# Expert stage of a routed mixture: the down product of a block placed behind the next block's up product

## What is computed there

```python
def expert_block(args):
    tok, e = args
    xb = xt[tok]
    g = xb @ w_gate[e] + b_gate[e]
    u = xb @ w_up[e] + b_up[e]
    g = jnp.minimum(g, SWIGLU_LIMIT)
    u = jnp.clip(u, -SWIGLU_LIMIT, SWIGLU_LIMIT)
    act = (u + 1) * (g * jax.nn.sigmoid(SWIGLU_ALPHA * g))
    return act @ w_down[e] + b_down[e]
```

## Time and profile before

| | us |
|---|---|
| median of 3 runs (lowest 4122.18, highest 4126.77) | 4125.26 |
| the profiled execution, device time | 4122.54 |
| its span in the trace | 4120.8 |
| TensorE busy over the span (83%) | 3426.4 |
| VectorE busy over the span (48%) | 1973.6 |
| expert stage, from the first gate product to the last down product | 838 to 2091 |

### The profile page before, as it was taken

The page is one execution under the profiler, slowest core; times in us unless marked ns, Lnnn a source line. Parts: engine busy times, 40 slices in busy tenths (PEclk is TensorE's granted clock), DMA queues, the critical chain, the costliest instruction groups (busy, mean ns, idle before and its releaser), DMA issues. The chain is left out here.

```text
span 4120.8 us, 37527 instructions
## 1 busy us (share of the span) xinstructions
PE 3426.4 (83%) x11876; PEld 1539.3 (37%) x11877; DVE 1973.6 (48%) x4086; ACT 659.6 (16%) x1532; POOL 932.9 (23%) x811
## 2 busy tenths in 40 slices
PE   7988998587899979999869845778788788888876
PEld 3345443332233323333335434544333233333332
DVE  5834223422333232232244055656666767667676
ACT  1011121000000000000022111412222222222212
POOL 2000000102222221021220040003444444444443
PEclk9999999699999989999989966899999999999998
DMA  9825333469999995597972000038999999999997
GB/s 333 284 87 200 137 115 114 188 229 408 376 364 366 364 412 233 215 363 283 385 262 98 27 0 0 1 150 345 421 415 412 421 408 408 422 403 422 417 421 327
DMA packets 194149, 1157.36 MB, mean 281 GB/s; under 512 B 25659, under 2 KB 27995, under 8 KB 74356
## 3 DMA queue, kind: packets, MB, share of 16 engines
q1 hardware_dynamic: 97140, 565.17, 35.3%
q0 software_dynamic: 80576, 564.05, 33.5%
q10 hardware_dynamic: 16320, 26.75, 2.1%
HBM read 1128.96 MB, written 48.68 MB: 286 GB/s over the span
## 5 line engine op out<-in xcount | busy, mean ns | idle before, releaser
L2462 DVE SCALAR_TENSOR_TENSOR mod<-q_uv,mix 128x1024 f32<-128x1024 f32 x512 | 627.1, 1225 | 391.5 <-DMA q_uv<-in_peer_uv,q_picks 387.0
L1149 PE MATMUL ps<-wt,e_xT 128*64 128x512 f32 x3200 | 729.4, 609 | 97.7 <-DMA wt<-in_w_exp 96.9
L2167 POOL DMA_INDIRECT q_uv<-in_peer_uv,q_picks x512 | 569.5, 1112 | 1053.9 <-PE ps L2259 720.8
L2259 PE MATMUL ps<-q_uv,q_dg 128*128 128x512 f32 x1024 | 518.7, 663 | 144.5 <-ACT q_dg L2336 144.5
L2259 PE MATMUL ps<-q_uv,tri 128*128 128x512 f32 x1024 | 465.4, 608 | 81.3 <-ACT tri L2336 81.3
L1129 POOL COPY wt<-e_land 128x2048 f32<-128x2048 f32 x124 | 237.7, 1917 | 1019.4 <-DMA e_land<-in_w_exp 1019.4
L1149 PEld LDWEIGHTS ps<-wt,e_xT 128*64 128x64 f32 x3200 | 236.9, 140 | 580.5 <-issue 430.0
L2259 PEld LDWEIGHTS ps<-q_uv,q_dg 128*128 128x128 f32 x1024 | 213.1, 213 | 441.1 <-issue 441.1
L1149 PE MATMUL ps<-wt,e_aT 128*64 128x512 f32 x1600 | 356.0, 597 | 21.5 <-ACT e_aT L1202 21.5
L2259 PEld LDWEIGHTS ps<-q_uv,tri 128*128 128x128 f32 x1024 | 194.9, 194 | 348.0 <-issue 347.9
L454 PE MATMUL ps<-hT,wt 128*128 128x512 f32 x640 | 285.1, 602 | 1.5 <-DVE wt L781 1.5
(11 more groups left out here) (439 smaller groups left out, 3402.7 us busy)
## 6 DMA issues: line engine op xcount, KB each, us to landing
wt<-in_w_exp SPq DMA_DIRECT2D x260, 1024.0 KB, 17.5
e_land<-in_w_exp SPq DMA_DIRECT2D x124, 1024.0 KB, 24.4
wt<-in_w_in_units SPq DMA_DIRECT2D x15, 2048.0 KB, 11.1
mod<-in_w_mod_units SPq DMA_DIRECT2D x48, 512.0 KB, 5.8
scratch_xs<-const_zeros SPq DMA_DIRECT2D x8, 2080.0 KB, 9.4
mod<-in_w_ada_units SPq DMA_DIRECT2D x32, 512.0 KB, 7.5
p_ring<-in_w_in SPq DMA_DIRECT2D x7, 2048.0 KB, 10.6
e_xg<-scratch_xs ACTq DMA_DIRECT2D x104, 128.0 KB, 7.3
```

The source lines that it names most:

```text
L1149: ins = nc.tensor.matmul(ps[64 * h:64 * h + 64, at, :], lhs[:, k % 4, 64 * (k // 4):64 * (k // 4) + 64], wt[:, u, a, h * W:(h + 1) * W], s ...
L2167: pool.indirect_dma_start(out=uv[:, n % NR, :, :].rearrange("p a d -> p (a d)"), out_offset=None, in_=A["peer_uv"], in_offset=bass.Indirec ...
L2259: last = nc.tensor.matmul(acc(t)[:, c, :], dg(n), uv[:, n % NR, 1, c * W:(c + 1) * W], start=fresh, stop=closing)
L2462: dve.scalar_tensor_tensor(junk[:, n % 2, :], uv[:, n % NR, 0, :], 1.0, mix[:, tile_of(k), :], ALU.mult, ALU.mult, accum_out=ap[:, k % 2, ...
```

## The change

Two orders are rewritten and nothing else. TensorE's loop body does the up product of block i before the down product of block i-1:

```diff
                             turn(AT, ut, s_at)
                             pe.wait_ge(s_xg, i * 32 + 64)
                             turn(XT, xg, s_xt)
+                            up(e, b)
                             down(i - 1, before)
-                            up(e, b)
```

```diff
                     dve.tensor_scalar(gt[:, :], gt[:, :], LIMIT, None, ALU.min).then_inc(s_g, 1)
+                    dve.wait_ge(s_mm[7], i * 2 + 4)
+                    dve.wait_ge(s_g, i + 2)
+                    dve.sem_inc(s_go, 1)
+                    link(dve.tensor_tensor(ut[:, :], ps[:, U, :], bias[:, 1, :], ALU.add))
+                    link(dve.tensor_scalar(ut[:, :], ut[:, :], LIMIT, -LIMIT, ALU.min, ALU.max))
+                    link(dve.scalar_tensor_tensor(ut[:, :], ut[:, :], 1.0, gt[:, :], ALU.add, ALU.mult))
+                    dve.wait_ge(s_sig, i + 1)
+                    dve.tensor_tensor(ut[:, :], ut[:, :], sg[:, :], ALU.mult).then_inc(s_act, 1)
                     if not first:
                         scaled(i - 1)
                         dve.wait_ge(s_y, i + 1)
                     dve.sem_inc(s_dve, 1)
                     count[0] += 1
-                    dve.wait_ge(s_g, i + 2)
-                    dve.sem_inc(s_go, 1)
                     dve.stream_shuffle(bias[:, 2, :], raw[:, 2, :], [0] * 32).then_inc(s_shuf, 1)
-                    dve.wait_ge(s_mm[7], i * 2 + 4)
-                    link(dve.tensor_tensor(ut[:, :], ps[:, U, :], bias[:, 1, :], ALU.add))
-                    link(dve.tensor_scalar(ut[:, :], ut[:, :], LIMIT, -LIMIT, ALU.min, ALU.max))
-                    link(dve.scalar_tensor_tensor(ut[:, :], ut[:, :], 1.0, gt[:, :], ALU.add, ALU.mult))
-                    dve.wait_ge(s_sig, i + 1)
-                    dve.tensor_tensor(ut[:, :], ut[:, :], sg[:, :], ALU.mult).then_inc(s_act, 1)
```

## The result

The changed kernel takes 4239.41 us (median of 4 runs, 4238.54 to 4241.59), the kernel before 4126.02. The ratio is 1.0277, with a 95% interval from 1.0259 to 1.0295: 113.4 us slower, where 100.9 was forecast.

A forecast was written before the change was run, and what follows sets the result against it. By turns DMA pace (one-block experts) or TensorE (many-block experts) bounds the kernel. 92.3 + 4.6 + 4.0 - 2.1 + 2.1 = +100.9 us on 4125.3 gives 4226.2; range 4185 to 4262.

The forecast's parts named there:

- The restart: DMA engines, where a several-block expert gives way to the next: up units issued 6.44 us later, behind the s_shuf wait.
- the place of the up product: TensorE, second expert after a several-block one: up product, now next to its weights, waits for them; 3.8 us per change.
- The nine changes: From a several-block expert over one or more one-block experts to the next several-block one: 9 x 10.26 = 92.3 us slower.
- M straight to M: Two places where one several-block expert directly follows another: 2 x 2.3 = 4.6 us slower.
- the start: First blocks of the expert stage: spreading of the down bias stands behind the whole up chain; 4.0 us slower.
- The end: Last blocks of the expert stage: weights land later, but the 5.78 us activation wait is covered; 2.1 us slower.
- The clock: TensorE's new waits at the up product, under 2 us, keep the full clock; nothing in the sum.
- that rival: Half clock: up products waiting for their last quarter run partly at 1.2 GHz, 13 places, up to +43 us; 15%.
- The rival on the other side: Faster: up units go out as freed, from 9.8 us after the last block's gate starts; about -20 us, 4105; 4%.
- inside the large experts: Five block periods without waits, each 0.43 us shorter as the wait for ScalarE's copy is covered; 2.1 us gained.

The follow-up runs named there:

- experiment 1: Kernel before with TensorE's order untouched, only the spreading of the down bias (raises s_shuf) moved to the end of VectorE's body: 4207.75 us, ratio 1.0203.
- experiment 2: Changed kernel with SyncE issuing the four up units ahead of the s_shuf wait and biases: 4121.83 us, ratio 0.9998 to the kernel before.
- Experiment 4: Changed kernel with the block loops of TensorE, ScalarE and VectorE cut from 62 possible blocks to 50: 4233.68 us in one execution.
- experiment 5: Changed kernel with GpSimd waiting on s_shuf and issuing the biases, SyncE issuing all units without that wait: 4100.93 us, ratio 0.9939 to the kernel before.

## Why the prediction was right

**The restart.** The step that carried the sum was that SyncE's wait on s_shuf already binds and moves with the down product. It is shown from both sides. With the wait late and the products untouched, the cost is its length (experiment 1). With the wait gone from ahead of the up units and the products as changed, 107.4 of 112.1 us disappear (experiment 2), the place of the up product included, since its weights then come sooner. The forecast had the up units at T+26.0; they go out at T+25.75.

**The nine changes.** 10.26 was forecast for each and 10.0 measured, and the split fits what was argued: 6.2 restart, by experiment 1, and a remainder of 3.8 for the place of the up product. One time on the way was written wrong, without effect on the sum: the last up unit of E2 is issued at 1735.46, which is T+44.9 and not T+45.2; T+66.1 follows from 44.9. Within the runs of one-block experts nothing moved (33.0 us at 410 and 412 GB/s).

**M straight to M, and the start.** Right in kind, 2.3 forecast against 3.6 for each, and 4.0 against 6.2. The term that was mis-sized is the landing of the four up units: 12.2 us from the first issue to the last landing were taken from rows 7, and it is 13.7 in the changed kernel. The rows (up units issued from 1782.23):

```profile
DMA to landing us min/median/max: 4.8/8.0/12.1
```

The last was issued at 1783.83 and landed 12.1 us later, at T+39.4 instead of T+38.2; in the two straight changes the slowest landing was 12.0 and 12.2, and at the stage's start it is 14.3 from the first issue (858.86) to the last quarter (873.19). Two things are new there. The rows' load of block i+2 (two DMAs of 128 KB from ScalarE, issued at 1786.48) falls among the four units, and these are issued within 1.6 us of each other instead of 3.1. TensorE's new order is not needed for it: in experiment 1, which has both of these and the old order, the slowest of the four took 12.3. Which of the two it is was not tested.

**The end.** Forecast 2.1, measured 10.8: the one step that failed. TensorE's wait of 5.78 us for the last activation is covered, as I wrote, but I took the place behind it for free. In the sum the empty turns of TensorE and of ScalarE stand at nothing. In the kernel before they fit into that same wait (5.78 against 3.71), so they were probably hidden there; no run took them out of the kernel before. In the changed kernel TensorE's show as 3.7 us of issue behind the down product, ScalarE's stand between its last store, which now comes late, and the last copy, and with these two gaps the lower clock at the last product stayed. Experiment 4 takes 6.4 of the 8.7 us away by taking the empty turns out. The remaining 2.3 include ScalarE's store, which now comes just ahead of the copy.

**The clock.** The forecast left it out, and for the changed kernel that was right where it counts: the waiting up quarters take 1.94 us except at the stage's start, where two take 2.57 and 2.71. Most gates of the one-block experts did lose the clock behind their waits of 3.6 (9.95 instead of 7.04 at 1808.33), but the up quarters behind them still waited for weights (0.54 to 1.23), so it cost nothing there. The price I had given to that rival exists, but elsewhere: 1.7 us in experiment 2 behind a wait of 2.07. The rule of the Trainium skill that I set against the forecast ("TensorE: Matmul & The Clock Gate", section "HAM oscillation — how this bites in real kernels") is about products shorter than the waits for their weights. Here it did not speak against the forecast: up units that land 3.0 us apart leave waits of about 1.1 between quarters of 1.94.

**The rival on the other side** named the right lever. Its arithmetic, the next T at T+69.3 and about 20 us below the kernel before, was met only when biases and down units were freed as well (69.8 to 70.0, 22.5 us below, experiment 5). With only the up units ahead of the wait, as it was worded, it came out at no change (experiment 2).

**The rest.** Forecast and result differ by 12.5 us in the medians. 8.7 of them are the end, 2.7 the changes straight to the next M, 2.2 the start, less 2.0 for the nine changes and 0.4 inside the large experts: 11.2.

## What to carry to other kernels

Before a product is moved, follow not only its buffers but every wait that stands in order on the queue which refills them: weights that are free 7 us sooner are worth nothing if the same queue first waits for something the move has made later. When a transfer queue can run dry, the time that counts is that of the first refill's issue, and a small transfer with a wait of its own (here 24 KB of biases) belongs on another queue than the 8 MB of up and down weights that stand behind it. A chain's place next to its loads is a cost of its own: work that used to stand between loading and use was hiding the landing.

## What the runs showed that I had not expected

A loop's skipped turns are not free where they come to lie on the path. For 12 blocks that do not exist, TensorE lost 3.7 us and ScalarE's copy came 4.4 after its store instead of 0.4. In the kernel before there was a longer wait for something else at this place, which could cover both.

TensorE's clock fell behind shorter waits than in the rows read before the prediction, and already in the kernel before:

```profile
1187.66 7.07 PE L1149 MATMUL ps<-wt,e_xT 128*64 128x512 f32 x24 [2.01 <-DMA wt<-in_w_exp]
```

The first quarter of this gate took 3.46 us. In the traces of all nine kernels, no quarter of a gate or up product behind a wait of 1.30 to 1.92 us lost the clock (83 of them). Of 40 behind waits of 1.93 to 2.22, 18 took 2.40 to 3.63 instead of 1.94 and 22 did not. So at 2 us of waiting the same wait goes either way, and what decides was not settled here. The Trainium skill ("TensorE: Matmul & The Clock Gate", section "HAM oscillation — how this bites in real kernels") says that products shorter than the waits between them lose the clock. With a quarter's 1.94 as the product, the quarters of experiments 2 and 5 (waits of 2.07 and 1.67) both agree. Two things do not agree: 15 quarters behind waits of 1.95 to 2.22 kept the clock, and 16 of 18 gates of the changed kernel lost it behind waits of 3.60 to 3.64, though the product ahead of them takes 7.04.
